# Three places of a streaming-encoder kernel: last head's outputs ahead of the scaling of the states, first head's logarithm halves and key turn ahead, GpSimd's products for two slabs held back

## The chip, the cores and the metric

The kernel runs on one core of a Trainium2 chip. The metric is the device time of one execution in microseconds. It is given as the median of three runs, and one further execution was profiled. The engines are PE (TensorE, matrix multiplies and transposes), DVE (VectorE), ACT (ScalarE), POOL (GpSimd) and SP (SyncE, which issues all the DMAs here).

## The reference

One step of a two-layer encoder over 512 prompt rows and 128 sample rows (8 streams of 16 rows), width 1024. Layer A is gated linear attention with 4 heads (key width 128, value width 256); layer B is latent attention with 8 heads. The change touches layer A and the first steps of layer B:

```python
proj = rmsnorm(x, norm_pre) @ w_in                       # q, k, v, gate, glr
g = log_sigmoid(glr @ w_gate2 + b_gate) / 16
# per head; chunked along the rows
b = cumsum(g); qe = q * exp(b); kd = k * exp(-b)
scores = where(causal, qe @ kd.T, 0)
o = scores @ v + qe @ S                                  # S: state that comes in
S_new = exp(b_last) * S + (k * exp(b_last - b)).T @ v    # an output
o = rmsnorm(o, head_norm) * silu(gate)
x = x + rmsnorm(o @ w_out, norm_post)
# then the shared latent of layer B
ckv = rmsnorm(rmsnorm(x, kv_norm) @ kv_w_down[:, :256], kv_latent_norm)
```

The 128 sample rows have a state of their own per stream and head (`state_gla`), which is loaded, used, updated and stored.

## The kernel before

The program is written by hand. A list `STEPS` gives the order of the work. Every step has a name and a tuple of engines that take part in it (`PARTS`). Every engine walks through the same list in the same order and does its own part of each step in which it has one. So an instruction that has to wait holds up everything that stands behind it on its engine. The waits between engines are written out (`after(engine, who, step)`); every engine counts its finished steps in a semaphore.

All matrices are split into a high and a low half (`_hi`, `_lo`), and one product is three matmuls (`mm3`: L1563, L1564, L1565, hi*hi, lo*hi, hi*lo). A high half is written by ACT (a copy, L991), the low half by DVE (a subtraction, L1260), from the same source. Weights come in pieces of 128x1024 through a ring of four staging buffers; a piece is split by ACT and DVE into a slab, and where a norm's gain belongs to the weight, POOL first multiplies it in (L924, step `piece`).

PSUM is used as 8 banks. The steps of PE take them in turn (`bank_numbers`), and a step waits until the banks it gets have been read out by the step that had them before (`before_bank`).

The steps by name, for head `h` (0 to 3):

- `z`, `ln`, `lg`, `lgh`: the gate's logarithm in five parts (heads 0 to 3, and part 4 for the sample rows). `ln` is ACT's logarithm (L1052), `lg` is DVE's (L1326), `lgh` splits the result (ACT L991 `lg_hi`, DVE L1260 `lg_lo`). `c h` on PE sums them up along the rows (L1646, L1647) and needs `lgh h`. `g0 t` is the first head's gate for row tile `t` (PE, then tanh on ACT L1043, then a product on DVE L1315). `em` and `e 0` on ACT make exp(-b) and exp(b).
- `q`, `qlo`, `k`, `klo`: q and k times their exponentials (DVE L1342, L1256 `kt`) and their halves. `kT` turns k on PE (L1664), and its halves are `kn_hi`, `kn_lo`. `sc` is the scores, `sclo` their low half. `U` is the prompt's state update (a chain of seven instructions on DVE), `Slo` the low half of the states (`st_lo`, DVE L1260).
- `o` is the output of the four prompt tiles (PE, 21 matmuls), `os` that of the sample tile (PE L1703 reads the states `st_s`). For both ACT sums the squares (L1121, L1123), POOL takes the power (L945 to L948), DVE scales (L1422, L1423).
- `Us h j` (j = 0, 1) is the update of the sample states: PE L1686, DVE adds it to `st_s` (L1256), ACT scales `st_s` (L1127, eight instructions in all). `sts` stores `st_s`. It may overwrite `st_s` only when `os` has read it.
- In the last head the gate is made late, tile by tile: `gl t` (48 matmuls for two tiles, tanh on ACT L1101; tiles 0 and 1 then take one product on DVE, L1376; tiles 2 to 4 take two, L1378 and L1256 `rows<-rows,st_in`, the second with both inputs in SBUF). `oT t` turns the finished rows (PE L1610), and `y` multiplies them by the output weights `wo A`. `ldr` loads the input rows again.
- `lcn` norms the latent rows (DVE L1460), `gb 3` is a slab of layer B.

In the last head the list before reads: `sc`, `sclo`, `U`, `Slo`, `gl 0`, `gl 1`, the pieces of `wo A 0`, `os`, `Us 0`, `Us 1`, `sts`, `o`, `ldr`, `gl 2`, `gl 3`, `oT 0`, `gl 4`, `oT 1` to `oT 4`, the pieces of `wo A 1`.

## Time and profile before

| | |
|---|---|
| median of 3 runs | 646.67 us (646.52 to 646.95) |
| profiled execution | 644.79 us |
| its span, first to last instruction | 643.0 us |
| PE busy | 617.9 us (96%), 4714 matmuls |
| DVE, ACT, POOL busy | 383.2, 315.8, 125.3 us |
| mean granted clock of PE | 0.994 of full |

The profiled execution's span is 1.8 us shorter than its own time; what lies outside of the span is not part of the program's work. PE's row says how full the engine is, not how well it runs: a matmul's record lasts longer than the distance to the next one, since they are pipelined. The granted clock is the share of full speed (2.4 GHz) that PE was given; 0.5 is 1.2 GHz.

### The profile page before, as it was taken

To read this page: it belongs to the slowest core of one execution; us is meant where nothing else is said; L and a number is where in the kernel's file an instruction comes from. 1 tells how busy PE (TensorE), PEld (TensorE's weight loads), DVE (VectorE), ACT (ScalarE), POOL (GpSimd) and SP (SyncE) were. 2 spreads that over 40 slices of the span, in tenths; PEclk is the share of its full clock that TensorE was granted. 3 is DMA by queue.
4 is the path that set the end of the run, shared out by engine and by line. 5 is a ranking of instruction groups with operands and counts; after the bars stand their busy time and mean duration, and the time that the engine had idled before them with its cause. 6 is when DMAs were issued, how large, how long until landed. Compare 5 with 4: busy or idle time off the path is not lost.

```text
span 643.0 us, 12101 instructions
## 1 busy us (share of the span) xinstructions
PE 617.9 (96%) x4714; PEld 596.3 (93%) x4714; DVE 383.2 (60%) x574; ACT 315.8 (49%) x618; POOL 125.3 (19%) x140
## 2 busy tenths in 40 slices
PE   8998999999999879999999999999999999999996
PEld 7998999999999779999999999989999888899996
DVE  5475667355454674238664567557778877773415
ACT  6786464442462553236435433355555668872311
POOL 0110010010030152216425410211000118650001
PEclk9999999999999989999999999999999999999998
DMA  8923262270262262234234420321001046766004
GB/s 301 345 82 92 90 199 73 87 215 28 74 197 67 74 229 66 86 87 173 67 93 112 127 66 2 114 70 47 34 18 50 13 151 209 252 196 229 2 1 165
DMA packets 66281, 73.69 MB, mean 115 GB/s; under 512 B 8112, under 2 KB 58544, under 8 KB 66096
## 3 DMA queue, kind: packets, MB, share of 16 engines
q1 hardware_dynamic: 66224, 72.91, 35.8%
q8 instruction: 38, 0.62, 0.4%
q14 instruction: 19, 0.16, 0.1%
HBM read 62.12 MB, written 10.78 MB: 113 GB/s over the span
## 4 chain that ended last, share of the span: by engine, by line
PE 65%; DVE 15%; ACT 10%; issue 4%; DMA 3%; POOL 2%; SPq 1%; DVEq 0%; ACTq 0%; POOLq 0%
PE bank L1563 21%; PE bank L1564 20%; PE bank L1565 20%; DVE slab_lo L1260 2%; DMA x_nat<-in_x_sample_dram 2%; ACT prob L1194 2%; DVE pT_lo L1260 2%; ACT slab_hi L991 1%; PE bank L1610 1%; DVE sT_lo L1260 1%; ACT sT_hi L991 1%; ACT qS L991 1%; DVE stat L1540 1%; DMA x_raw<-in_xT_dram 1%; DVE rows L1256 1%
## 5 line engine op out<-in xcount | busy, mean ns | idle before, releaser
L1563 PE MATMUL bank<-slab_hi,hat_hi 128*128 128x256 f32 (+2 forms) x600 | 171.0, 285 | 3.8 <-DVE rows L1423 1.8
L1564 PE MATMUL bank<-slab_lo,hat_hi 128*128 128x256 f32 (+2 forms) x600 | 169.8, 283 | 0.0
L1565 PE MATMUL bank<-slab_hi,hat_lo 128*128 128x256 f32 (+2 forms) x600 | 169.8, 283 | 0.0
L1563 PEld LDWEIGHTS bank<-slab_hi,hat_hi 128*128 128x128 f32 x600 | 115.2, 192 | 5.0 <-DVE rows L1423 2.0
L1564 PEld LDWEIGHTS bank<-slab_lo,hat_hi 128*128 128x128 f32 x600 | 115.2, 192 | 0.0
L1565 PEld LDWEIGHTS bank<-slab_hi,hat_lo 128*128 128x128 f32 x600 | 115.2, 192 | 0.0
L1260 DVE TENSOR_TENSOR slab_lo<-stage,slab_hi 128x1024 fp32r<-128x1024 f32 (+3 forms) x70 | 84.8, 1212 | 24.9 <-ACT slab_hi L991 23.4
L1563 PE MATMUL bank<-hat_hi,slab_hi 128*128 128x320 f32 x256 | 79.8, 312 | 0.9 <-DVE rows L1487 0.8
L1565 PE MATMUL bank<-hat_hi,slab_lo 128*128 128x320 f32 x256 | 79.1, 309 | 0.0
L1564 PE MATMUL bank<-hat_lo,slab_hi 128*128 128x320 f32 x256 | 79.1, 309 | 0.0
L991 ACT ACTIVATE slab_hi<-stage 128x1024 fp32r<-128x1024 f32 (+3 forms) x70 | 71.0, 1014 | 10.2 <-issue 3.6
L1563 PEld LDWEIGHTS bank<-hat_hi,slab_hi 128*128 128x128 f32 x256 | 48.1, 188 | 1.4 <-DVE rows L1487 1.4
L1564 PEld LDWEIGHTS bank<-hat_lo,slab_hi 128*128 128x128 f32 x256 | 48.1, 188 | 0.0
L1565 PEld LDWEIGHTS bank<-hat_hi,slab_lo 128*128 128x128 f32 x256 | 48.1, 188 | 0.0
L1565 PE MATMUL bank<-slab_hi,oT_lo 128*128 128x256 f32 x160 | 45.3, 283 | 0.0
L1563 PE MATMUL bank<-slab_hi,qS 128*128 128x256 f32 x128 | 36.5, 285 | 0.0
L1564 PE MATMUL bank<-slab_lo,qS 128*128 128x256 f32 x128 | 36.2, 283 | 0.0
L945 POOL TENSOR_TENSOR stat<-stat,stat 128x1 f32<-128x1 f32 (+1 forms) x8 | 2.3, 287 | 171.4 <-ACT junk L1123 136.3
L1138 ACT ACTIVATE junk<-bank 128x256 bf16<-128x256 f32 x26 | 9.7, 383 | 50.4 <-PE bank L1565 50.4
L971 POOL TENSOR_TENSOR skL<-stage,skS 128x512 fp32r<-128x512 f32 x8 | 14.6, 1827 | 92.2 <-ACT skS L991 92.2
L1565 PEld LDWEIGHTS bank<-slab_hi,oT_lo 128*128 128x128 f32 x160 | 30.7, 192 | 0.0
L1194 ACT ACTIVATE prob<-bank,stat 128x512 f32<-128x512 f32 (+3 forms) x32 | 16.6, 523 | 19.4 <-DVE stat L1521 19.1
(340 smaller groups left out, 1434.2 us busy)
## 6 DMA issues: line engine op xcount, KB each, us to landing
stage<-in_a_w_in_dram SPq DMA_DIRECT2D x22, 512.0 KB, 5.2
stage<-in_b_w_in_dram SPq DMA_DIRECT2D x10, 512.0 KB, 3.8
st_s<-in_state_gla_dram SPq DMA_DIRECT2D x4, 1024.0 KB, 6.7
out_dram<-st_s SPq DMA_DIRECT2D x4, 1024.0 KB, 4.9
stage<-in_a_w_out_dram SPq DMA_DIRECT2D x8, 512.0 KB, 4.3
stage<-in_ckvT_dram SPq DMA_DIRECT2D x8, 512.0 KB, 4.1
stage<-in_cache_ckv_dram SPq DMA_DIRECT2D x8, 512.0 KB, 4.0
stage<-in_b_w_out_dram SPq DMA_DIRECT2D x8, 512.0 KB, 3.5
```

The costliest lines, as they stand in the source:

```text
L945: link(pool.tensor_tensor(r, s, S1(("rrm",), stat2)[:, t:t + m], MUL))
L971: last = pool.tensor_tensor(skL[b][:, :], staged_as(kind, step), raw(skS[b][:, :]), SUB)
L991: return act.activation(out, in_, ACT.Copy)
L1138: last = act.activation(junk[:, i * 256:(i + 1) * 256], row[:, i * 256:(i + 1) * 256], ACT.Square, accum_out=S1(("y", ph, t), t=s))
L1194: last = act.activation(prob[u][:, c0:c0 + i + 1, :], bank[:, j, 0:(i + 1) * P].rearrange("p (s n) -> p s n", n=P), ACT.Exp, bias=S1(("S", ...
L1256: return dve.tensor_tensor(out, a, b, op)
L1260: return dve.tensor_tensor(lo, full, raw(hi), SUB)
L1540: last = dve.reduce_max(S1(("ss", b), stat2), row[:, 0:TOK], AX.X, negate=True)
L1563: pe.matmul(out, a[0], b[0], start=first, stop=False)
L1564: pe.matmul(out, a[0], b[1], start=False, stop=False)
L1565: return pe.matmul(out, a[1], b[0], start=False, stop=last)
L1610: last = pe.transpose(row[:, k * P:(k + 1) * P], rows[:, t, k * P:(k + 1) * P], ident)
```

## The change

Three places of the order are written anew.

1. In the first head, the halves of the logarithm of heads 2, 3 and 1 move ahead (`lgh 2`, `lgh 3`, `lgh 1`), and so do `q 0` and `qlo 0`; the first piece of `qk 1` moves behind them, and the turn of the key (`kT 0`) stands ahead of `c 2`.
2. In the last head, PE does `Us 0`, `Us 1`, `o`, `os`, `gl 2` where it did `os`, `Us 0`, `Us 1`, `o`, `gl 2`. ACT's part of `Us` becomes a step of its own, `Ux`, and stands behind `o`, `os` and `gl 2` in the last head (in the other heads it stays where it was). DVE's part of `Us` gets a wait for PE's `os`.
3. POOL gets two waits: ahead of the products for `wo A 1` it waits for DVE's `gl 3`, ahead of those for `gb 3` for DVE's `lcn`.

```diff
--- before.py
+++ after.py
@@ -132,9 +132,9 @@
     out += [("rq",), ("rr",), ("const",), ("piece", ("qk", 0), 0), ("gf",), ("gfh",), ("gfl",), ("plo", ("qk", 0), 0), ("vg", 0), ("gw",)]
     out += [("vg", 1), ("vg", 2), ("g0", 0), ("g0", 1), ("g0", 2), ("glT",), ("g0x", 0), ("g0x", 1), ("piece", ("qk", 0), 1)]
     out += [("z", u) for u in Z_ORDER] + [("g0x", 2), ("qp", 0), ("plo", ("qk", 0), 1)]
-    out += [("ln", 0), ("lg", 0), ("ln", HA), ("lg", HA), ("ln", 2), ("lg", 2), ("lgh", 0), ("lgh", HA), ("ln", 3), ("lg", 3), ("ln", 1), ("lg", 1)]
-    out += [("g0", 3), ("g0", 4), ("c", 0), ("em",), ("e", 0), ("lgh", 1), ("piece", ("qk", 1), 0), ("q", 0), ("lgh", 2), ("lgh", 3), ("qlo", 0), ("k", 0), ("klo", 0)]
-    out += [("c", 1), ("c", 2), ("kT", 0), ("c", 3)]
+    out += [("ln", 0), ("lg", 0), ("ln", HA), ("lg", HA), ("ln", 2), ("lg", 2), ("lgh", 0), ("lgh", HA), ("ln", 3), ("lg", 3), ("ln", 1), ("lgh", 2), ("lg", 1), ("lgh", 3)]
+    out += [("g0", 3), ("lgh", 1), ("g0", 4), ("c", 0), ("em",), ("e", 0), ("q", 0), ("qlo", 0), ("piece", ("qk", 1), 0), ("k", 0), ("klo", 0)]
+    out += [("c", 1), ("kT", 0), ("c", 2), ("c", 3)]
     out += [("lds", 0)]
     for h in range(HA):
         last = h + 1 == HA
@@ -150,13 +150,13 @@
             out += [("gl", t) for t in range(EARLY_GATE)] if last else []
             load(("wo", "A", 0) if last else ("qk", h + 1))
             out += [] if last else [("gt", h), ("gts", h)]
-        out += [("os", h), ("Us", h, 0), ("Us", h, 1), ("sts", h)]
         if last:
-            out += [("o", h), ("ldr",)]
-            out += [("gl", t) for t in range(EARLY_GATE, NT - 1)] + [("oT", 0), ("gl", NT - 1)]
+            out += [("Us", h, 0), ("Us", h, 1), ("o", h), ("os", h), ("gl", EARLY_GATE), ("Ux", h, 0), ("Ux", h, 1), ("sts", h), ("ldr",)]
+            out += [("gl", t) for t in range(EARLY_GATE + 1, NT - 1)] + [("oT", 0), ("gl", NT - 1)]
             out += [("oT", t) for t in range(1, NT)]
             load(("wo", "A", 1))
         else:
+            out += [("os", h), ("Us", h, 0), ("Us", h, 1), ("Ux", h, 0), ("Ux", h, 1), ("sts", h)]
             load(("v", h + 1))
             out += [("o", h), ("lds", h + 1)]
     project_out(out, load, "A")
@@ -288,7 +288,7 @@
     "q": ("dve", "act"), "k": ("pe", "dve", "act"), "qlo": ("dve",), "klo": ("dve",),
     "v": ("pe", "act", "dve"), "vs": ("pe", "act", "dve"), "kT": ("pe", "act", "dve"), "sc": ("pe", "dve", "act"),
     "sclo": ("dve",), "gt": ("pe", "act", "dve"), "gts": ("pe", "act", "dve"), "U": ("pe", "dve", "act"),
-    "Slo": ("dve",), "os": ("pe", "act", "pool", "dve"), "o": ("pe", "act", "pool", "dve"), "Us": ("pe", "dve", "act"),
+    "Slo": ("dve",), "os": ("pe", "act", "pool", "dve"), "o": ("pe", "act", "pool", "dve"), "Us": ("pe", "dve"), "Ux": ("act",),
     "oT": ("pe", "act", "dve"), "y": ("pe", "act", "dve"), "ys": ("pe", "act", "dve"), "r": ("pool", "dve"),
     "rx": ("pool", "dve"), "lc": ("pe", "act", "dve"), "lcn": ("pool", "dve"), "gl": ("pe", "act", "dve"), 
     "cn": ("act", "dve"), "cT": ("pe", "act", "dve"), "qa": ("pe", "act", "dve"), "qas": ("pe", "act", "dve"),
@@ -846,7 +846,7 @@
                     sp.dma_start(st_s[:, :, :], dram["state_gla"][0, :, h].rearrange("b k v -> k b v")).then_inc(state_in, 16)
                 elif kind == "sts":
                     h = step[1]
-                    after(sp, "act", "Us", h, 1)
+                    after(sp, "act", "Ux", h, 1)
                     sp.dma_start(st_sample[0, :, h].rearrange("b k v -> k b v"), st_s[:, :, :]).then_inc(state_out, 16)
                 elif kind == "stp":
                     h = step[1]
@@ -854,7 +854,7 @@
                     sp.dma_start(st_prompt[0, 0, h], st_in[:, 0, :]).then_inc(final_out, 16)
                 elif kind == "ldr":
 
-                    for who, s in (("act", ("Us", HA - 1, 1)), ("act", ("o", HA - 1)), ("pe", ("Us", HA - 1, 1))):
+                    for who, s in (("act", ("Ux", HA - 1, 1)), ("act", ("o", HA - 1)), ("pe", ("Us", HA - 1, 1))):
                         after(sp, who, *s)
                     sp.dma_start(x1[:, 0:NP, :], dram["x_prompt"][0].rearrange("(t p) d -> p t d", p=P)).then_inc(rest_in, 16)
                     sp.dma_start(x1[:, NP, :], dram["x_sample"].rearrange("b l d -> (b l) d")).then_inc(rest_in, 16)
@@ -917,6 +917,10 @@
                 if kind == "piece":
                     _, name, j = step
                     n = STAGED_NO[step]
+                    if name == ("wo", "A", 1):
+                        after(pool, "dve", "gl", EARLY_GATE + 1)
+                    if name == ("gb", 3):
+                        after(pool, "dve", "lcn")
                     pool.wait_ge(stage_in[STAGE_OF[n]], STAGE_COUNT[n])
                     pool.wait_ge(gains_in, 16 * (len(gain) - 1))
                     for i, (w, k0, k1, c0, cols, g) in enumerate(SLABS[name][j]):
@@ -1121,8 +1125,9 @@
                         last = act.activation(junk[:, t * DV:(t + 1) * DV], row[:, t * DV:(t + 1) * DV], ACT.Square, accum_out=S1(("o", step[1]), t=t))
                 elif kind == "os":
                     last = act.activation(junk[:, 0:DV], row[:, 0:DV], ACT.Square, accum_out=S1(("o", step[1]), t=NP))
-                elif kind == "Us":
+                elif kind == "Ux":
                     _, h, j = step
+                    after(act, "dve", "Us", h, j)
                     for b in range(4 * j, 4 * j + 4):
                         last = act.activation(st_s[:, b, :], st_s[:, b, :], ACT.Copy, scale=Ep[:, SEQ + b * SL + SL - 1:SEQ + (b + 1) * SL])
                 elif kind == "qs":
@@ -1412,6 +1417,7 @@
                 elif kind == "Us":
                     _, h, j = step
                     dve.wait_ge(state_in, 16 * (h + 1))
+                    after(dve, "pe", "os", h)
                     v = st_s[:, 4 * j:4 * j + 4, :]
                     last = tt(v, row.rearrange("p (b n) -> p b n", n=DV), v, ADD)
                 elif kind in ("o", "os"):
```

PE in the last head, from behind `gl 1` on (`st_s,q_own` is `os`, `v_own` is `Us`, `vv` with `scT` is the first part of an output). Before:

```order
L1703 MATMUL bank<-st_s,q_own 32x256 x8
L1563 MATMUL bank<-vv_hi,scT_hi 128x256
L1564 MATMUL bank<-vv_lo,scT_hi 128x256
L1565 MATMUL bank<-vv_hi,scT_lo 128x256
L1686 MATMUL bank<-v_own_hi,kn_hi 128x512 x2
L1686 MATMUL bank<-v_own_lo,kn_hi 128x512 x2
L1686 MATMUL bank<-v_own_hi,kn_lo 128x512 x2
L1686 MATMUL bank<-v_own_hi,kn_hi 128x512 x2
L1686 MATMUL bank<-v_own_lo,kn_hi 128x512 x2
L1686 MATMUL bank<-v_own_hi,kn_lo 128x512 x2
L1563 MATMUL bank<-vv_hi,scT_hi 128x256
L1564 MATMUL bank<-vv_lo,scT_hi 128x256
```

and of the change, from the same place on:

```order
L1692 MATMUL bank<-v_own_hi,kn_hi 128x512 x2
L1692 MATMUL bank<-v_own_lo,kn_hi 128x512 x2
L1692 MATMUL bank<-v_own_hi,kn_lo 128x512 x2
L1692 MATMUL bank<-v_own_hi,kn_hi 128x512 x2
L1692 MATMUL bank<-v_own_lo,kn_hi 128x512 x2
L1692 MATMUL bank<-v_own_hi,kn_lo 128x512 x2
L1569 MATMUL bank<-vv_hi,scT_hi 128x256
L1570 MATMUL bank<-vv_lo,scT_hi 128x256
L1571 MATMUL bank<-vv_hi,scT_lo 128x256
L1569 MATMUL bank<-vv_hi,scT_hi 128x256
L1570 MATMUL bank<-vv_lo,scT_hi 128x256
L1571 MATMUL bank<-vv_hi,scT_lo 128x256
```

`os` (eight matmuls and the first three with `scT`) is gone from here; `Us` comes at once, the prompt's outputs follow it, and `os` stands behind them, ahead of `gl 2`.

ACT in the last head, from the scores' half on (`junk,stat` are the sums of squares: x4 is `o`, the single one `os`; `st_s` is the scaling of the states; `st_in<-bank` and `Em<-bank` are the tanh of `gl`). Before:

```order
L991 ACTIVATE st_hi<-st_in 128x768
L1101 ACTIVATE Em<-bank,stat_68 128x256 x2
L991 ACTIVATE slab_hi<-stage_51 128x1024
L991 ACTIVATE slab_hi<-stage_52 128x1024
L1123 ACTIVATE junk,stat<-bank 128x256
L1127 ACTIVATE st_s<-st_s,Ep 128x256 x8
L1121 ACTIVATE junk,stat<-bank 128x256 x4
L1101 ACTIVATE st_in<-bank,stat_68 128x256 x2
L991 ACTIVATE hat_hi<-bank 128x8x128
L1101 ACTIVATE st_in<-bank,stat_68 128x256
L991 ACTIVATE hat_hi<-bank 128x8x128 x4
```

and of the change:

```order
L995 ACTIVATE st_hi<-st_in 128x768
L1105 ACTIVATE Em<-bank,stat_68 128x256 x2
L995 ACTIVATE slab_hi<-stage_51 128x1024
L995 ACTIVATE slab_hi<-stage_52 128x1024
L1125 ACTIVATE junk,stat<-bank 128x256 x4
L1127 ACTIVATE junk,stat<-bank 128x256
L1105 ACTIVATE st_in<-bank,stat_68 128x256
L1132 ACTIVATE st_s<-st_s,Ep 128x256 x8
L1105 ACTIVATE st_in<-bank,stat_68 128x256
L995 ACTIVATE hat_hi<-bank 128x8x128
L1105 ACTIVATE st_in<-bank,stat_68 128x256
L995 ACTIVATE hat_hi<-bank 128x8x128 x4
```

The eight scalings stood ahead of the squares of `o`; now they stand behind both squares and behind the tanh of `gl 2`, and ahead of that of `gl 3`.

DVE in the first head (`lg_lo` is `lgh`, `z_min` is `lg`, `rows<-rows,bank` is `g0`, `tmp`, `q_own` and `qT_lo` are `q` and `qlo`, `slab_lo` is the piece, `kt` is `k`). Before:

```order
L1260 TENSOR_TENSOR lg_lo<-z_min,lg_hi 128x512 x2
L1326 SCALAR_TENSOR_TENSOR z_min<-bank,z_abs 128x512 x2
L1315 SCALAR_TENSOR_TENSOR rows<-rows,bank 128x256 x2
L1260 TENSOR_TENSOR lg_lo<-z_min,lg_hi 128x512
L1260 TENSOR_TENSOR slab_lo<-stage_49,slab_hi 128x1024
L1342 SCALAR_TENSOR_TENSOR tmp<-bank,Ep 128x640
L1348 COPY q_own<-tmp 128x4x16 x2
L1260 TENSOR_TENSOR lg_lo<-z_min,lg_hi 128x512 x2
L1260 TENSOR_TENSOR qT_lo<-tmp,qT_hi 128x640
L1256 TENSOR_TENSOR kt<-bank,Em 128x640
L1260 TENSOR_TENSOR kT_lo<-kt,kT_hi 128x640
```

and of the change:

```order
L1331 SCALAR_TENSOR_TENSOR z_min<-bank,z_abs 128x512
L1265 TENSOR_TENSOR lg_lo<-z_min,lg_hi 128x512
L1331 SCALAR_TENSOR_TENSOR z_min<-bank,z_abs 128x512
L1265 TENSOR_TENSOR lg_lo<-z_min,lg_hi 128x512
L1320 SCALAR_TENSOR_TENSOR rows<-rows,bank 128x256
L1265 TENSOR_TENSOR lg_lo<-z_min,lg_hi 128x512
L1320 SCALAR_TENSOR_TENSOR rows<-rows,bank 128x256
L1347 SCALAR_TENSOR_TENSOR tmp<-bank,Ep 128x640
L1353 COPY q_own<-tmp 128x4x16 x2
L1265 TENSOR_TENSOR qT_lo<-tmp,qT_hi 128x640
L1265 TENSOR_TENSOR slab_lo<-stage_49,slab_hi 128x1024
L1261 TENSOR_TENSOR kt<-bank,Em 128x640
```

The last two `lg_lo` stood between q's product and q's low half; now all stand ahead of `q`, and the slab's half stands behind `qT_lo`.

## Rows read from the trace of the kernel before

**Rows 1.** Waits of PE: which line waited for which, us, times, longest

```profile
PE bank L1610 <- DVE rows L1423: 4.3, 1, 4.3
```

**Rows 2.** Stretches: busy PE, PEld, DVE, ACT, POOL; granted clock, DMA share, GB/s

```profile
217.00:229.00 12.00, 6.80 (x55) 6.39 (x53) 4.48 (x7) 5.93 (x18) 4.14 (x9) 1.00 0.62 183
229.00:233.00 4.00, 3.04 (x15) 3.07 (x16) 3.86 (x7) 1.01 (x1) 3.84 (x3) 0.57 1.01 386
233.00:360.00 127.00, 126.23 (x1042) 125.39 (x1040) 69.53 (x84) 54.24 (x124) 48.87 (x49) 1.00 0.33 102
```

**Rows 3.** Timeline of PE in the last head: start, us, instruction, idle before

```profile
212.17 1.07 PE L1703 MATMUL bank<-st_s,q_own 128*32 128x256 f32 x16
...
213.72 0.53 PE L1686 MATMUL bank<-v_own_hi,kn_hi 32*128 32x512 f32 x4
...
215.04 0.36 PE L1563 MATMUL bank<-vv_hi,scT_hi 128*128 128x256 f32 x1 [0.33 <-DVE rows L1376]
...
219.62 0.39 PE L1563 MATMUL bank<-slab_hi,hat_hi 128*128 128x256 f32 x1 [1.83 <-DVE rows L1423]
...
225.35 0.28 PE L1565 MATMUL bank<-slab_hi,hat_lo 128*128 128x256 f32 x1
...
229.96 0.66 PE L1610 MATMUL bank<-const,rows 128*128 128x128 f32 x2 [4.33 <-DVE rows L1423]
...
238.60 0.39 PE L1563 MATMUL bank<-slab_hi,hat_hi 128*128 128x256 f32 x1
```

**Rows 4.** Timeline of DVE in the last head

```profile
213.07 0.96 DVE L1260 TENSOR_TENSOR st_lo<-st_in,st_hi 128x768 fp32r<-128x768 f32 x1 [1.04 <-ACT st_hi L991]
...
219.60 2.48 DVE L1256 TENSOR_TENSOR st_s<-bank,st_s 128x1024 f32<-128x1024 f32 x2
228.15 0.88 DVE L1422 SCALAR_TENSOR_TENSOR rows<-bank,stat,rows 128x256 f32<-128x256 f32 x2 [6.07 <-POOL stat L948]
...
230.30 2.10 DVE L1256 TENSOR_TENSOR rows<-rows,st_in 128x256 f32<-128x256 f32 x1
...
232.89 1.54 DVE L1256 TENSOR_TENSOR rows<-rows,st_in 128x256 f32<-128x256 f32 x1
...
236.34 0.43 DVE L1256 TENSOR_TENSOR rows<-rows,st_in 128x256 f32<-128x256 f32 x1
237.32 5.00 DVE L1260 TENSOR_TENSOR hat_lo<-bank,hat_hi 128x1024 fp32r<-128x1024 f32 x4 [0.56 <-ACT hat_hi L991]
```

**Rows 5.** Timeline of ACT in the last head

```profile
220.92 3.45 ACT L1127 ACTIVATE st_s<-st_s,Ep 128x256 f32<-128x256 f32 x8 [4.24 <-DVE st_s L1256]
```

**Rows 6.** Timeline of POOL behind the last head

```profile
228.25 7.93 POOL L924 TENSOR_TENSOR stage<-stage,gain_a_head_norm 128x1024 f32<-128x1024 f32 x4 [0.22 <-POOL stat L948]
```

**Rows 7.** Timeline of PE in the first head

```profile
48.76 0.36 PE L1563 MATMUL bank<-hat_hi,slab_hi 128*128 128x320 f32 x1
...
57.42 0.30 PE L1646 MATMUL bank<-const_r,lg_hi 128*128 128x130 f32 x1 [0.34 <-ACT lg_hi L991]
...
59.91 0.41 PE L1664 MATMUL bank<-const,kt 128*128 128x128 f32 x2 [1.19 <-DVE kt L1256]
...
64.26 0.36 PE L1563 MATMUL bank<-vv_hi,kn_hi 128*128 128x256 f32 x1 [0.78 <-DVE kn_lo L1260]
```

**Rows 8.** Timeline of ACT in the first head

```profile
45.14 1.28 ACT L1043 ACT_TABLE_LOAD   x1
...
50.52 0.20 ACT L1071 ACTIVATE decay<-bank 128x2 f32<-128x2 f32 x1
...
55.89 1.29 ACT L991 ACTIVATE lg_hi<-z_min 128x512 fp32r<-128x512 f32 x2
```

**Rows 9.** Timeline of DVE in the first head

```profile
47.01 0.42 DVE L1315 SCALAR_TENSOR_TENSOR rows<-rows,bank 128x256 f32<-128x256 f32 x1 [0.65 <-ACT rows L1043]
...
52.61 1.23 DVE L1260 TENSOR_TENSOR slab_lo<-stage,slab_hi 128x1024 fp32r<-128x1024 f32 x1 [0.43 <-ACT slab_hi L991]
...
58.94 0.82 DVE L1256 TENSOR_TENSOR kt<-bank,Em 128x640 f32<-128x640 f32 x1
```

## The prediction

> **What bounds the kernel now.** I read the waits of PE first. PE is busy for 96% of the span, so a microsecond that PE waits is a microsecond of the kernel, if nothing later takes it back. The longest wait of all is the turn of the last head's rows (L1610), which waits 4.3 us for DVE's scaling of the outputs (L1423) [rows 1].
>
> The timeline of PE at that place shows three waits between `gl 1` and the output product `y`: 0.33, 1.83 and 4.33 us [rows 3]. The tags are a little short: `gl 2` and `gl 3` are 48 matmuls from 219.62 to 225.35, 0.12 us apart, while one is recorded for 0.28 us. Each wait so costs 0.16 us more than its tag.
>
> The stretches show what the long wait does besides. From 229 to 233 us the granted clock is 0.57 where it is 1.00 before and after [rows 2]; with the two levels that is some 3.4 us at 1.2 GHz. PE was idle before the clock fell, and had work again from 229.96, so about 2.9 us of work ran at half speed, and 1.4 us were lost.
>
> Why DVE is late is in the timelines of DVE and ACT. The states' scaling (eight instructions, 220.92 to 224.37) stands on ACT ahead of the squares of `o` [rows 5]. From the first square (224.4) over POOL to DVE's scaling at 228.15 go 3.75 us [rows 4]. PE had finished `o` at about 217.7.
>
> In the first head PE waits three times: 0.34 before `c 2`, 1.19 before the key's turn, 0.78 before `U` [rows 7]. The turn waits for `kt`, which DVE starts at 58.94 [rows 9], although PE's `k 0` (from 48.76, 48 matmuls of 0.147) is done by 56.0: halves of the logarithm and of q stand ahead of it.
>
> **The last head, on the clock of the trace before.** PE: `Us` comes at 212.17 and takes 0.8 (213.72 to 215.04 without the wait of 0.33 + 0.16). `o` then needs `st_lo`, which ends at 214.03 [rows 4]; so PE waits from 213.0 to 214.2. This is a new wait of 1.2 us: `os` (212.17 to 213.72) used to lie over it. `o` is 21 matmuls, to 216.8. `os` takes 1.55 as before, to 218.3. `gl 2` and `gl 3` take 2.9 each, to 224.1.
>
> ACT sums the squares of `o` from 217.0, and 3.75 us later, at 220.8, DVE could scale. DVE does `Us` first, which now waits for PE's `os`: 218.4 to 220.9 (2.48, `st_s`). Behind it in DVE's queue are only `o`, `os` and the `gl`. `o` is scaled from 220.9 to 222.6 (the 1.7 of 228.15 to 229.8). PE asks for it at 224.1, with 1.5 us to spare. So both waits of 1.83 and 4.33 go: `gl 2` takes a bank that is long free, and `oT 0` finds its rows.
>
> What is late next is ACT. After the tanh of `gl 2` (221.9) come the scalings, 3.45 us, to 225.4, and only then the tanh of `gl 3`; DVE has `gl 3` at 226.9. PE needs it only for `oT 2`, at about 228.8. The store of the states and the load of the input rows, issued by SP behind the scalings, move 1 us later; the rows are used after all four slabs of `y`, so this costs nothing.
>
> POOL's products for `wo A 1` now start behind `gl 3`, at 227.05. Each takes 1.98 (four in 7.93 [rows 6]), so they end at 229.0, 231.0, 233.0 and 235.0. The last two are those of `wo A 2`, which queue behind. `wo A 1` is needed by PE behind 120 matmuls of `y`, at about 247, so the hold itself is covered by some 10 us even after both halves are made.
>
> But it moves a collision. The product of `gl` with both inputs in SBUF takes 0.43 with POOL at rest, and took 2.10 and 1.54 beside POOL's products; it ended at 232.40 and 234.43, each 0.2 behind the end of a product of POOL (228.25 plus two or three times 1.98) [rows 4, 6]. `gl 2` and `gl 3` now run with POOL at rest. `gl 4` does not: PE has it at 227.9, its tanh ends at 228.6, and the product starts at 229.15, in POOL's second product. I take 231.2 for its end. `oT 4`, ready on PE at 230.6, starts at 231.35. DVE's half of `oT 1` (1.25 of the row of four [rows 4]) follows at 232.45, and `y`, which gets its bank, starts at 232.6. It started at 238.60: **6.0 us** less. Bounds for this term: 7.0 if `gl 4`'s product falls between two of POOL's (`y` then at 231.6), and 4.6 if the clock falls nevertheless.
>
> The Trainium skill bears on this place: "SBUF — State Buffer", section "Who interferes with whom", says that a DVE instruction with two SBUF inputs and a GpSimd instruction that reads SBUF exclude each other for a whole instruction, whoever is first. The two rows agree, since both products ended just behind one of POOL's. By that rule the hold does not remove the collision but hands it to `gl 4`, and speaks against this part of the change; by a slowing in proportion (0.43 to 1.54) the product of `gl 4` would end at 230.7 and the sum would gain another 0.5.
>
> **The first head.** On ACT two halves (1.29 for two) now stand ahead of the table load (45.14, 1.28) and the tanh behind it [rows 8]. DVE's `g0 3`, which ended at 47.43, ends 1.3 later, at 48.7, and `k 0` on PE, whose bank it frees, starts at 48.86 instead of 48.76: a new wait of 0.1. ACT has slack behind that, and `e 0`, which ended at 50.7, ends at about 51.1. DVE's `q` follows (0.8 and two copies, to 52.3), its high half on ACT, its low half to 54.1, the slab's half (1.23) to 55.6. So DVE is free when PE ends `k 0` at 56.1, and `kt` is there at 57.0, 2.8 us earlier. PE is then at the end of `c 1` (57.05) and turns the key without a wait; `c 2` and `c 3` (1.1 each) lie over the halves of k, which end at 58.8, and `sc` starts at 59.95. `kn_lo` is done at 60.4, before `sc` ends at 61.6. So all three waits go: 0.34 + 1.19 + 0.78 + 3 x 0.16 = 2.8, less 0.1 for `k 0` and 0.1 behind `c 1`: **2.6 us**. Bounds: 2.8, and nothing, if ACT's new order makes `k 0` as late as it makes `sc` early.
>
> **`gb 3`** held behind `lcn`: nothing. PE works 126.23 of the 127 us from 233 to 360 [rows 2]; DVE's `lcn` gets shorter under cover, and the products start about when they did.
>
> **Sum.** 6.0 + 2.6 = 8.6 us. The profiled execution goes from 644.79 to 636.2. The median of the runs lies 1.9 us above the profiled time, so it goes from 646.67 to **638.0** (1.3% less). 0.2% (1.3 us) is about what a measurement can tell from no change.
>
> **The rivals.**
> - The clock falls nevertheless, or ACT's scalings ahead of `gl 3` stop PE at `oT 2`. For it: a new wait of 1.2 us at 213, and only 2 us between `gl 3` on DVE and `oT 2`. Against: it stayed at 1.00 from 217 to 229, with a wait of 1.83 in it. The last head then gives 4 to 4.6: 639.8. Chance 0.14.
> - The first head gives nothing: the later tanh delays `k 0`, or q's chain still keeps `kt` back. For it: ACT and DVE pass six halves to each other there, and 0.5 us between the slab's half and `kt` is all there is. Against: the halves that move were waited for by nobody at their new place. Time 640.6. Chance 0.09.
> - The waits come back: PE reaches a place earlier that something else fixes, a transfer above all. For it: the loads of weights are issued when a stage is free, and the rows' load runs beside. Against: none of PE's longer waits is for a DMA. Time 645.4 to 646.7. Chance 0.03.
> - Slower: PE, which now works from 65 to 290 us with almost no stop, is granted less clock in the output products. Each microsecond at 1.2 GHz costs 0.5, so from 17 us of it on the kernel gets slower; 22 us give 649. For it: the only fall of the clock in mid-kernel stands here. Against: it came behind a stop, and 127 us of nearly unbroken work follow at 1.00 [rows 2]. Chance 0.04.
>
> **How the numbers follow.** Both gains as summed: 0.70, time 638.0, its own range 636.8 to 639.2 (1.0 for the collision, 0.2 for how runs differ). Down to 636.3 the range takes in a missed collision with waits worth somewhat more; up to 640.6 it takes in the first two rivals. Faster 0.93, same 0.03, slower 0.04.
>
> **What would show it.** In the profile after: no wait of L1616 (the old L1610) for DVE's scaling, and the clock at 1.00 all through the head; a wait of about 1 us for `st_lo` at `o`; the product of `gl 4` at 2 us and that of `gl 2` and `gl 3` at 0.43; `kt` less than 0.2 ahead of PE's turn and no wait at `U`; `y` 8.6 us earlier than 238.60. I am wrong if ACT reaches the tanh of `gl 3` later than 227, if the clock falls anywhere between 213 and 232, or if `k 0` waits more than 0.5 us.

## The result

The median of the kernel before is 646.6 us (six runs) and that of the changed one 636.33 us (six runs, of which one, a disturbed one of 1539.64 us, is left out of the ratio): the ratio is 0.984 (0.9826 to 0.9853), 10.3 us less. I had forecast 638.0, 8.6 us less. The gain is larger than my sum by 1.7 us, and the time stands at the very edge of my range of 636.3 to 640.6, which reached down that far for another reason (a collision that does not come). On another chip it was 647.4 against 636.35 (0.9826, 0.9808 to 0.9844).

The two profiled executions are 644.79 and 636.63 us, 8.2 apart. So in the traces my sum is nearly met (8.2 for 8.6), and what I missed is not in them. The spans are 643.0 and 634.8.

PE has two waits left in the last head of the changed kernel:

```profile
PE bank L1569 <- DVE st_lo L1265: 1.0, 1, 1.0
...
PE bank L1616 <- DVE rows L1261: 0.7, 1, 0.7
```

The 4.3 us for the scaling of the outputs [rows 1] and the 1.8 before `gl 2` are gone. In their place stand the two that the sum had put there: `o` waits for the states' low half, and the turn of tile 4 for the product of `gl 4`.

The stretches of the changed kernel over the first and the last head (busy time of PE, PEld, DVE, ACT, POOL, then the clock):

```profile
50.00:60.00 10.00, 10.00 (x78) 9.89 (x76) 5.31 (x9) 5.66 (x15) 0.00 (x0) 1.00 0.31 95
...
212.00:226.00 14.00, 14.00 (x127) 13.29 (x126) 10.28 (x16) 9.40 (x24) 4.49 (x9) 1.00 0.43 132
226.00:240.00 14.00, 13.17 (x110) 12.73 (x109) 9.82 (x8) 6.23 (x6) 7.74 (x5) 1.00 0.81 281
...
229.00:233.00 4.00, 3.90 (x33) 3.66 (x32) 3.90 (x4) 3.54 (x4) 3.16 (x2) 1.00 1.02 414
```

The clock is 1.00 in the first head and all through the last one, where it was 0.57 from 229 to 233 us [rows 2]. DMA traffic in those 4 us is as heavy as before (share 1.02 and 414 GB/s, against 1.01 and 386).

PE's timeline in the last head, which answers to [rows 3]:

```profile
209.52 0.52 PE L1692 MATMUL bank<-v_own_hi,kn_hi 32*128 32x512 f32 x4
...
211.53 0.36 PE L1569 MATMUL bank<-vv_hi,scT_hi 128*128 128x256 f32 x1 [1.04 <-DVE st_lo L1265]
...
214.20 0.42 PE L1709 MATMUL bank<-st_s,q_own 128*32 128x256 f32 x4
...
215.66 0.28 PE L1569 MATMUL bank<-slab_hi,hat_hi 128*128 128x256 f32 x1
...
221.41 0.27 PE L1616 MATMUL bank<-const,rows 128*128 128x128 f32 x1
...
228.66 1.06 PE L1616 MATMUL bank<-const,rows 128*128 128x128 f32 x8 [0.72 <-DVE rows L1261]
229.82 0.39 PE L1569 MATMUL bank<-slab_hi,hat_hi 128*128 128x256 f32 x1
```

`Us`, `o`, `os`, `gl 2` and `gl 3`, `oT 0` follow each other, with one stop ahead of `o`. The output product starts at 229.82 instead of 238.60, 8.8 us earlier; the sum had 8.6. By the sample outputs of the first head PE has 2.7 of this (70.22 against 72.88), so the last head gives 6.1; the sum had 6.0.

DVE and POOL at the same place (the three `rows<-rows,st_in` are the second products of `gl 2`, `gl 3`, `gl 4`). DVE:

```profile
216.31 2.48 DVE L1261 TENSOR_TENSOR st_s<-bank,st_s 128x1024 f32<-128x1024 f32 x2 [1.26 <-PE bank L1571]
218.82 0.88 DVE L1428 SCALAR_TENSOR_TENSOR rows<-bank,stat,rows 128x256 f32<-128x256 f32 x2
...
221.49 0.42 DVE L1261 TENSOR_TENSOR rows<-rows,st_in 128x256 f32<-128x256 f32 x1
...
223.81 0.42 DVE L1261 TENSOR_TENSOR rows<-rows,st_in 128x256 f32<-128x256 f32 x1
...
226.43 2.08 DVE L1261 TENSOR_TENSOR rows<-rows,st_in 128x256 f32<-128x256 f32 x1
```

and POOL's products, which now wait for `gl 3`:

```profile
224.36 7.87 POOL L928 TENSOR_TENSOR stage<-stage,gain_a_head_norm 128x1024 f32<-128x1024 f32 x4 [4.86 <-DVE rows L1261]
```

The outputs are scaled from 218.82, 2.6 us before PE asks for them at 221.41. The products of `gl 2` and `gl 3` take 0.42. That of `gl 4` takes 2.08 and ends at 228.51, 0.2 behind the end of POOL's second product as the row gives it (224.36 + 2 x 1.97), 0.28 by that product's own record, which ends at 228.23. The collision was moved, not removed.

In the first head PE no longer waits for `kt` ([rows 7] of before):

```profile
48.85 0.39 PE L1569 MATMUL bank<-hat_hi,slab_hi 128*128 128x320 f32 x1
...
57.20 0.30 PE L1670 MATMUL bank<-const,kt 128*128 128x128 f32 x1
...
61.63 0.33 PE L1569 MATMUL bank<-vv_hi,kn_hi 128*128 128x256 f32 x1
```

`k 0` starts 0.09 later, the key's turn 2.71 earlier, `U` 2.63 earlier. The sum had 0.1, 2.8 and 2.6.

### The profile page after: what moved, and what is told of

It reads as the page before. It is cut to its first block, busy times and chain, and to the rows that moved or that the text cites. A ratio compares the mean times of both kernels' runs of the same rounds, so it can differ in the third digit from the quotient of the medians.

```text
span 634.8 us, 12113 instructions
## 1 busy us (share of the span) xinstructions
PE 617.2 (97%) x4714; PEld 595.4 (94%) x4714; DVE 380.3 (60%) x574; ACT 315.8 (50%) x618; POOL 125.0 (20%) x140
## 4 chain that ended last, share of the span: by engine, by line
PE 69%; DVE 14%; ACT 8%; issue 3%; DMA 3%; POOL 2%; SPq 1%; DVEq 0%; ACTq 0%; POOLq 0%
PE bank L1569 22%; PE bank L1571 21%; PE bank L1570 21%; DVE slab_lo L1265 2%; DMA x_nat<-in_x_sample_dram 2%; DVE pT_lo L1265 2%; ACT prob L1199 2%; DVE rows L1261 1%; DVE sT_lo L1265 1%; ACT slab_hi L995 1%; ACT qS L995 1%; DVE stat L1546 1%; DVE hat_lo L1265 1%; DMA x_raw<-in_xT_dram 1%; PE bank L1760 1%
## 5 line engine op out<-in xcount | busy, mean ns | idle before, releaser
L1199 ACT ACTIVATE prob<-bank,stat 128x512 f32<-128x512 f32 (+3 forms) x32 | 16.6, 523 | 19.4 <-DVE stat L1527 19.2
```

The source lines that it names most:

```text
L1199: last = act.activation(prob[u][:, c0:c0 + i + 1, :], bank[:, j, 0:(i + 1) * P].rearrange("p (s n) -> p s n", n=P), ACT.Exp, bias=S1(("S", ...
```

## The experiments

Each kernel ran beside the kernel before on its chip. The medians of the kernel before were 648.2, 647.3, 647.4 and 647.1 us on the four chips. A run's clock is the mean granted clock over its span.

### The kernel before again

No edit.

> The kernel before, once more. Open is why the runs gained 10 us (646.6 to 636.3) while the two profiled executions are only 8.2 us apart (644.79 to 636.63). Theory CLOCK: in most executions of the kernel before the clock falls for longer at the last head's stop than it did in the profiled one (3.4 us of 1.2 GHz there). Then the runs have mean granted clocks from 0.994 down to about 0.991, and the time follows the clock with some 0.64 us for each 0.001. Theory ELSEWHERE: the runs' clocks are all at 0.994, and the 1.8 us between the profiled execution and the others has nothing to do with the clock. Time in both: 645.7 to 647.

Measured: 646.49 us, runs from 644.53 to 648.6. The 17 other runs of the same kernel on this chip have a median of 648.2, so medians of this kernel differ by 1.7 us with nothing changed. With all its other runs on three of the chips I have 58 executions of the kernel before, each with its clock:

| mean clock | runs | us |
|---|---|---|
| 0.994 | 6 | 644.53 to 645.38 |
| 0.993 | 5 | 645.8 to 646.23 |
| 0.989 and 0.990 | 12 | 645.98 to 647.2 |
| 0.987 and 0.988 | 17 | 646.74 to 649.07 |
| 0.982 to 0.985 | 18 | 647.8 to 649.97 |

The eleven runs on the fourth chip fit in (644.57 to 649.0 us, 0.994 to 0.984). The time follows the clock. The profiled execution (644.79, 0.994) belongs to the fastest tenth; the median run has 0.987. Theory CLOCK holds in this, but not in its sizes: a line through the 58 runs gives 0.35 us for each 0.001 where I had 0.64, and the clocks go down to 0.982 where I had 0.991. Where the clock falls in the other runs, this does not tell; I had placed it in the last head.

The mean clock is a coarse measure of lost time. It also counts a fall at the very end, where PE has nothing left to do: in the profiled execution of the changed kernel PE's last matmul ends at 628.8 and the clock falls at 631.25, which alone makes its 0.997. So the 0.997 and 0.999 of the changed kernel need not differ in lost time.

### The first head's part alone

```diff
+    out += [... ("ln", 3), ("lg", 3), ("ln", 1), ("lgh", 2), ("lg", 1), ("lgh", 3)]
+    out += [("g0", 3), ("lgh", 1), ("g0", 4), ("c", 0), ("em",), ("e", 0), ("q", 0), ("qlo", 0), ("piece", ("qk", 1), 0), ...]
+    out += [("c", 1), ("kT", 0), ("c", 2), ("c", 3)]
```

The three lines stand in place of those of the kernel before ("..." marks what is left out of a line).

> The kernel before with the first head's part of the change alone. My sum: 2.6 us less than before, on the same clock as before (0.991 to 0.994), so about 644.0. Theory CLOCK says that nothing of the unforeseen 1.7 us is here: 2.4 to 2.8 less. Rival: the unforeseen part comes from the first head, 4 us or more less.

Measured: 641.93 us. That is 4.6 under the 646.49 of the kernel before as an experiment and 6.3 under the 648.2 of its runs in between (0.9913, 0.9894 to 0.9931), with clocks from 0.992 to 0.996. In its trace PE is 2.8 us earlier from `U` on; the sum had 2.6:

```profile
61.49 0.33 PE L1563 MATMUL bank<-vv_hi,kn_hi 128*128 128x256 f32 x1
```

So the waits of this part are worth 2.6 to 2.8 (its profiled execution is 2.7 under that of the kernel before on the chip, both at 0.994), and its runs gain at least another 1.8. That spoke for the rival, and against my place for the missing clock.

### The last head's part alone

```diff
-        out += [("os", h), ("Us", h, 0), ("Us", h, 1), ("sts", h)]
+            out += [("Us", h, 0), ("Us", h, 1), ("o", h), ("os", h), ("gl", EARLY_GATE), ("Ux", h, 0), ("Ux", h, 1), ("sts", h), ("ldr",)]
```

with `Ux` as in the change, and without POOL's two waits.

> The kernel before with the last head's part alone, without the two holds of GpSimd. Theory CLOCK: 6 us of waits and work as in my sum, plus what the clock costs most runs beyond the profiled one, 1.8 us, so 7.5 to 8.5 us less (638 to 639), with a mean clock of 0.997 or more. Rival: only the 6 us of my sum (640.6). For the collision without the hold: the products of two slabs start at once behind the outputs' power, and the products of tiles 2, 3 and perhaps 4 run beside them.

Measured: 641.47 us (0.9909, 0.989 to 0.9928), 5.0 under the 646.49 and 6.7 under the 648.2, with clocks from 0.989 to 0.994, none at the 0.997 of the expectation. Its trace shows why. The clock is whole in the last head, and broken in the first (stretches of PE: busy, clock, DMA share, GB/s):

```profile
45.00:60.00 15.00, 14.29 (x110) 1.00 0.28 85
60.00:71.00 11.00, 10.18 (x47) 0.53 0.30 97
71.00:90.00 19.00, 19.00 (x149) 1.00 0.25 78
```

From 60.6 to 70.9 PE works at 1.2 GHz: the 0.53 of 11 us. Its matmuls of 0.11 us' distance there come 0.21 apart:

```profile
63.95 0.41 PE L1565 MATMUL bank<-qT_hi,kT_hi 128*128 128x128 f32 x1
64.16 0.41 PE L1566 MATMUL bank<-qT_lo,kT_hi 128*128 128x128 f32 x1
```

Beside the trace of before, where this fall is absent, PE falls behind by 3.6 us between the key's turn and the sample outputs of this head. The two waits ahead of `c 2` and of the key's turn, which this variant still has (0.51 and 1.35 us by the distance of the matmuls), stand at the start of the fall: the second one lasts until 60.82, and the clock falls at 60.64, inside it. From the sample outputs of the first head to the output product this variant gains 6.5 us. That is the last head's term without the hold of POOL; with it the changed kernel has 6.1.

### Idle transposes in the waits of the first head

```diff
                 elif kind == "kT":
+                    if not step[1]:
+                        for _i in range(11):
+                            pe.transpose(row[:, 0:P], ident, ident)
                     after(pe, "dve", "k", step[1])
```

and seven more ahead of `U`'s wait for `kT`. They write into the bank that the step owns and overwrites.

> The kernel before, with 11 and 7 transposes of the identity that nobody reads in PE's waits before the key's turn and before the state update of the first head. No wait is taken away. Theory FIRST-CLOCK (new, from the run of the last head's part alone, whose profile has 10.2 us at 1.2 GHz from 60.6 us on): in many executions the three waits of the first head bring the clock down there, and that is what the change gave back beyond my sum. Then no run has a mean clock below 0.993, and the median falls to that of the undisturbed runs of before, 644.5 to 645.4, 1 to 3 us under the kernel before on the same chip. Theory WAITS-ONLY: filling the waits changes nothing, the spread stays at 0.984 to 0.994, same time.

Measured: 644.75 us median, 2.5 less than the 647.29 of the kernel before (0.9967, 0.9954 to 0.9981). Seven of nine runs lie between 0.992 and 0.994, two at 0.990 (646.3, 646.9), which the expectation had excluded; of the 20 runs before beside it only three are above 0.990. No wait was removed: the state update `U` starts at 64.00, where it started at 63.99 and 64.26 in the two traces of the kernel before. The stretches of its trace:

```profile
55.00:65.00 10.00, 9.65 (x82) 1.00 0.55 180
65.00:80.00 15.00, 15.00 (x122) 1.00 0.24 73
215.00:240.00 25.00, 20.30 (x145) 0.86 0.55 190
```

The first head is whole, and the last head's fall is there still. FIRST-CLOCK holds, with a rest: in this very trace (0.993) the last head has two falls of 3.4 us, at 220.9 and 231.2, where the profiled execution of before has one, and the two runs at 0.990 must have more somewhere. The wait of 0.51 ahead of `c 2` was not filled, so it does not bring the fall about by itself. In the two traces that show the fall (the last head's part alone, and the next experiment) it begins at 60.4 and 60.6, ahead of `U`, and PE then has no wait left at `U`; so of the two waits that were filled, the one ahead of the key's turn is the likelier cause. The two were not filled one by one.

### Idle transposes in the long wait of the last head

```diff
+                        if t == 0:
+                            for _i in range(34):
+                                pe.transpose(row[:, 0:P], ident, ident)
                         after(pe, "dve", *(("gl", t) if t >= EARLY_GATE else ("o", HA - 1)))
```

> The kernel before, with 34 idle transposes (3.7 us) in PE's long wait at the last head. The wait stays, the clock should not fall at 229 us. My term for this clock was 1.4 us: the output product starts 1.4 us earlier after the same wait, the profiled time goes from 644.6 to 643.2, and the mean clock of the best runs from 0.994 to 0.997. If the clock there costs nothing (its work was hidden), same time. The spread from the first head stays: runs from 0.987 to 0.997.

Measured: 647.15 us, no change in the median (0.9993, 0.9971 to 1.0015); the two best runs have 0.997 and 643.87 and 643.88, the worst 0.983 and 651.52. The clock of the last head is kept, but the first head's fall still varies by more than this is worth. In its trace that one lasts 6.8 us, from 60.4 on.

### Both fillings

The edits of the two kernels above together.

> The kernel before with both fillings. FIRST-CLOCK: all runs at 0.996 or more, spread under 1 us, median 643.1 to 643.5, that is 4 to 5 us under the kernel before on the same chip, though every wait is still there. WAITS-ONLY: at most 1.4 us under it.

Measured: 643.98 us, 3.3 under the kernel before on the same chip (0.995, 0.9933 to 0.9967); all six clocks at 0.996 to 0.998. The clocks are as expected, the times are not quite: I had 4 to 5 us less and a spread under 1 us, and the runs go from 643.65 to 645.79, two of them 1.9 us apart at the same 0.997. So part of the spread is not the clock, and I have no cause for it. The timeline of PE, with the 34 transposes in the wait:

```profile
225.29 3.88 PE L1608 MATMUL bank<-const 128*128 128x128 f32 x34
229.72 1.09 PE L1613 MATMUL bank<-const,rows 128*128 128x128 f32 x8 [0.56 <-DVE rows L1423]
230.57 0.36 PE L1563 MATMUL bank<-slab_hi,hat_hi 128*128 128x256 f32 x1
```

The waits are all there, the clock is whole up to PE's last matmul, and 3.3 us are gained. That is the share of the clock alone. The last head's part of it is 0.8 between the medians (643.98 against 644.75, whose runs overlap), where I had reckoned 1.4. At full clock `gl 4` and `oT 0` are shorter by that, but then the turns of the other tiles wait for DVE, whose products POOL still holds up: the output product starts at 237.75 instead of 238.60, and 0.7 of this arises behind `Us`.

### The changed kernel without the two holds of GpSimd

```diff
-                    if name == ("wo", "A", 1):
-                        after(pool, "dve", "gl", EARLY_GATE + 1)
-                    if name == ("gb", 3):
-                        after(pool, "dve", "lcn")
```

> The changed kernel without the two holds of GpSimd. If the hold is what makes the last head fast: slower than the changed kernel by 1 us or more, with a wait of PE at the turn of tile 2 or 3. By my working it only moves the collision: without it, GpSimd's four products start 4 us earlier, are done near the time of tile 4's product, and the kernel is as fast as the changed one or up to 0.8 us faster (635.5 to 636.4).

Measured: 636.11 us. Now POOL starts at 219.27 and DVE's products are:

```profile
221.03 0.42 DVE L1257 TENSOR_TENSOR rows<-rows,st_in 128x256 f32<-128x256 f32 x1
...
223.34 2.12 DVE L1257 TENSOR_TENSOR rows<-rows,st_in 128x256 f32<-128x256 f32 x1
...
227.20 0.43 DVE L1257 TENSOR_TENSOR rows<-rows,st_in 128x256 f32<-128x256 f32 x1
```

`gl 3` is hit instead of `gl 4`, where nobody waits for it. PE's first `Us` and the output product:

```profile
209.05 0.52 PE L1688 MATMUL bank<-v_own_hi,kn_hi 32*128 32x512 f32 x4
...
228.94 0.39 PE L1565 MATMUL bank<-slab_hi,hat_hi 128*128 128x256 f32 x1
```

The output product starts 0.9 us earlier than in the changed kernel (229.82), but `Us` is 0.5 earlier already (209.52 there), where no hold has acted yet. From `Us` to the output product are 19.9 us against 20.3 (20.30 and 20.32 in the two traces of the changed kernel). So the first hold costs 0.4 in the trace; between the medians (0.2 us) it can't be told.

### The hold of one slab moved behind the last gate tile

```diff
-                        after(pool, "dve", "gl", EARLY_GATE + 1)
+                        after(pool, "dve", "gl", NT - 1)
```

> The changed kernel with GpSimd's products for the output weights' second slab held back to behind the last gate tile instead of tile 3. If the collision that I forecast for tile 4's product costs PE time there (0.9 us by the profile after at the turn of tile 4, 0.3 at the output product), the product takes 0.43 us, both waits go, and the kernel is 1.0 us faster than the changed one: 635.2. If that slab then comes too late, slower.

Measured: 635.45 us median. The product of `gl 4` takes 0.42 here:

```profile
226.41 0.42 DVE L1261 TENSOR_TENSOR rows<-rows,st_in 128x256 f32<-128x256 f32 x1
```

and the output product comes 19.2 us behind `Us`, 1.1 sooner than in the changed kernel and 0.7 sooner than without holds:

```profile
209.49 0.52 PE L1692 MATMUL bank<-v_own_hi,kn_hi 32*128 32x512 f32 x4
...
228.66 0.39 PE L1569 MATMUL bank<-slab_hi,hat_hi 128*128 128x256 f32 x1
```

The three runs with clocks of 0.997 to 0.999 give 635.1 to 635.5; two more runs fell to 0.995 and 0.993 (636.8, 638.9). This is the fastest version that I have, 0.9 us under the changed kernel by medians from two chips. Its own runs spread over 3.8 us, so the gain rests on the trace.

### Without the hold of the gate slab of layer B

```diff
-                    if name == ("gb", 3):
-                        after(pool, "dve", "lcn")
```

> The changed kernel without the hold of GpSimd's products for the gate slab of layer B behind the latent's norm. PE has no wait there in either profile, so I expect the same time as the changed kernel within 0.3 us; only the five instructions of the norm on DVE take 6 us instead of 3 to 5. Rival: the hold is worth what the sum lacks, then 1 us or more slower.

Measured: 636.13 us, against 636.35 of the changed kernel on the same chip. It is worth nothing, as forecast.

### Sample outputs ahead of the prompt's

```diff
-            out += [("Us", h, 0), ("Us", h, 1), ("o", h), ("os", h), ("gl", EARLY_GATE), ...]
+            out += [("Us", h, 0), ("Us", h, 1), ("os", h), ("o", h), ("gl", EARLY_GATE), ...]
```

> The changed kernel with the sample tile's outputs ahead of the prompt's in the last head (states' updates, then os, then o). The wait of PE for the states' low half (1.19 us in the profile after) is then covered by os. By the rows: gl 2 starts 1.2 us earlier, the outputs' scaling is done just as PE asks for it, and the kernel is 1.0 to 1.3 us faster than the changed one. Rival: the power of os stands ahead of that of o on GpSimd and makes the scaling late, and the wait only moves to the turn of tile 0: same time.

Measured: 637.38 us, 1.0 slower than the changed kernel. `os` does cover the stop ahead of `o`, but `gl 2` now takes a bank of the states' update, and PE asks for it before DVE has read it:

```profile
PE bank L1569 <- DVE st_s L1261: 1.2, 1, 1.2
...
PE bank L1569 <- DVE rows L1381: 0.3, 1, 0.3
```

DVE does the halves of a weights' slab first:

```profile
212.71 2.49 DVE L1265 TENSOR_TENSOR slab_lo<-stage,slab_hi 128x1024 fp32r<-128x1024 f32 x2 [0.27 <-ACT slab_hi L995]
215.23 2.48 DVE L1261 TENSOR_TENSOR st_s<-bank,st_s 128x1024 f32<-128x1024 f32 x2
```

Part of the covered stop also comes back, as a wait of `o` for the product of `gl 1` (the 0.3). From `Us` to the output product are 21.1 us instead of 20.3. Neither of my theories had the bank in it.

### The same, with the slab's halves behind the sample outputs

```diff
-            load(("wo", "A", 0) if last else ("qk", h + 1))
+            load(("qk", h + 1)) if not last else None
...
-            out += [("Us", h, 0), ("Us", h, 1), ("o", h), ("os", h), ("gl", EARLY_GATE), ...]
+            out += [("Us", h, 0), ("Us", h, 1), ("os", h), ("piece", ("wo", "A", 0), 0), ("piece", ("wo", "A", 0), 1), ("o", h), ("gl", EARLY_GATE), ...]
...
-                        after(pool, "dve", "gl", EARLY_GATE + 1)
+                        after(pool, "dve", "gl", NT - 1)
```

The hold of POOL stands behind the last gate tile here too, as in the fastest version.

> The changed kernel with three edits in the last head: the sample tile's outputs ahead of the prompt's, the split of the first output weights' slab behind them (so that DVE updates the states at once and PE's banks come free), and the hold of GpSimd's products until behind tile 4's gate. In the run with os first alone, PE waited 1.38 us for the states' update to free a bank and 0.51 for tile 1's gate. If DVE's order is what made that wait, it goes: the stop for the states' low half (1.19) is replaced by 0.5, the turn of tile 4 does not wait, and the kernel is 1.6 to 1.9 us faster than the changed one: 634.4 to 634.8. Rival: the squares of o now wait on ACT behind the slab's halves, the outputs' scaling is late, and the turn of tile 0 waits: no better than with the hold alone (635.4).

Measured: 640.59 us, 5 us worse than the best. A piece of `wo A` is also a step of POOL, and I had moved it there too, behind the power of `os` (POOL, then ACT):

```profile
214.35 3.87 POOL L928 TENSOR_TENSOR stage<-stage,gain_a_head_norm 128x1024 f32<-128x1024 f32 x2
```

```profile
216.33 1.06 ACT L995 ACTIVATE slab_hi<-stage 128x1024 fp32r<-128x1024 f32 x1 [3.62 <-issue]
218.30 1.06 ACT L995 ACTIVATE slab_hi<-stage 128x1024 fp32r<-128x1024 f32 x1 [0.91 <-POOL stage L928]
219.40 0.38 ACT L1125 ACTIVATE junk<-bank 128x256 bf16<-128x256 f32 x1
```

POOL's two products, then ACT's halves, then the squares of `o`: these start at 219.40 instead of 214.37, and PE waits 4.0 us at the turn of tile 0, until 224.94. The rival held, more strongly than I had put it, since the halves themselves waited for POOL. The clock was at 1.2 GHz for 6.8 us from 223.4 on, inside the stop.

### The changed kernel again

No edit.

> The changed kernel once more, on the chip of this call. Theory FIRST-CLOCK: its runs lie close together, all with a mean clock of 0.997 or more, 635.7 to 636.6, while the kernel before on the same chip spreads over 2 to 4 us with its clocks from 0.984 to 0.994; the difference of the fastest runs of both is my sum, 8.6 us, and that of the medians 10 us or more.

Measured: 636.35 us, runs from 636.12 to 636.42, clocks 0.998 and 0.999; the nine runs before beside it spread from 646.23 to 648.74. Against the 0.994 runs of the kernel before (644.53 to 645.38) that is 8.1 to 9.3 us, and against the median on the same chip 11.0. The fastest runs of both on this chip are 10.1 apart, not the 8.6 that I expected: none of its nine runs of the kernel before was at 0.994.

## Why the prediction was right and wrong

**The failed step** is the last line of the sum: "The median of the runs lies 1.9 us above the profiled time, so it goes from 646.67 to 638.0". I took the 1.9 us for a constant that both kernels have. By the experiments it is the price of a fall of the clock in the first head which most executions of the kernel before have and the profiled one had not: 11 of 58 runs are at 0.993 or above, and with the first head's waits filled the median is 644.75, that of the profiled execution. The changed kernel does not have it, and its profiled execution (636.63) is not faster than its median. With the offset at zero the sum gives 636.2; measured was 636.3. That these agree so closely is partly luck: the two profiled executions are 8.2 apart and not 8.6, and the changed kernel's is 0.3 above its median. My 0.2 us "for how runs differ" had the same fault: it came from three runs within 0.4 us, and 58 runs go from 644.5 to 650.0.

The kinds of evidence are not equal. That the time follows the clock is shown by 58 runs. That the fall is at the first head is shown by two traces (10.2 and 6.8 us, at 60.6 and 60.4), both of variants that have the first head's order of before; no trace of the kernel before itself has caught it. That PE's waits there bring it about is shown by filling two of the three, which brings seven of nine runs to 0.992 and above and takes 2.5 us off the median. How often a run without any long stop falls all the same (two of five with the moved hold) was not followed up.

**The last head.** Right in mechanism and size. The waits at `gl 2` and `oT 0` went; `o` waits 1.04 by its tag for the states' low half, 1.2 with the 0.16 that the tags lack (I had 1.2); `gl 4` collides for 2.08 (I had 2.05, from 229.15 to 231.2). The clock there was mis-sized as a term of its own, 1.4 against 0.7 to 0.8 by the fillings. This did not touch the sum, which was made from one timeline.

**The rule of the exclusive lock** (the Trainium skill, "SBUF — State Buffer", section "Who interferes with whom") held for the blocked products in these traces: 2.10 and 1.54 before, 2.08 after, 2.12 without the hold, and 0.42 wherever POOL was at rest. Each blocked one ends 0.28 or 0.29 us behind the record of a product of POOL. Without the hold the product of `gl 2` started 0.14 us before the first product of POOL ended (221.03 against 221.17) and still took 0.42, so the last 0.14 us of that record held nobody up. As I had drawn from the rule, the hold hands the collision to `gl 4`. By the run without holds this part of the change costs 0.4 us in the trace; held one tile longer, it would gain 0.7 over no hold.

**The first head.** Right: 2.6 us of waits (2.63 at `U`). What I left out is that its waits were dearer than their length. I had priced the clock only where the one trace showed a fall.

**The rivals.** The clock did not fall at the new stop of 1.0 us in any of the traces that have it. The first head's part did not fail. Little came back later: the lead of 8.8 us at the output product is 8.2 at the end, and PE's waits behind it have grown by as much (those for `pT_lo` from 0.9 to 1.3, a new one of 0.3 for `qN_lo`). PE's longer unbroken work was not granted less: the mean clock is 0.997 to 0.999.

## What to carry to other kernels

Before you sum against a profile, ask how the profiled execution differs from the median of the runs. If the runs spread and their mean clocks differ, part of the time is a fall of the clock that the one trace may not show; short waits close together, each too small to look at, can be its cause, and filling them with idle transposes prices it without any other change. When a step is moved in a list that all engines share, follow it on every engine that has a part in it; here the bank and GpSimd were the ones that I forgot. And when two traces are compared, count from an instruction that the edit can't have touched: the first matmul of `k 0` starts anywhere from 48.31 to 49.67 us in the traces that have the order of before, and 0.5 us of such an offset made a cost of 0.4 look like 0.9.

## What the runs showed of the hardware

Two waits of 0.51 and 1.35 us with 1.1 us of work between them went with 6.8 and 10.2 us at 1.2 GHz in two traces, the fall beginning 0.2 us before the end of the second wait in one and 0.95 behind it in the other, and with none in two traces with the same waits (the profiled execution of before and its repeat). Behind the wait ahead of `gl 2` (1.83 us) the clock fell at 220.9 in the run with the first head filled, and in none of the five other traces with this wait. So the same program's clock differs from run to run, and here that was worth nearly 4 us (a mean of 644.8 at 0.994, of 648.5 at 0.984), more than most single edits of this document.
